# First pair's weight buffers refilled in halves, the last pair's up products ahead of the down products of the pair before, lambda and one GpSimd sum behind K's rotations

## The reference

```python
# first layer, differential attention
lam = exp(sum(lam_p[0] * lam_p[1])) - exp(sum(lam_p[2] * lam_p[3])) + lam_init
a = probs(q1, k1) - lam * probs(q2, k2)      # q and k normed and rotated (rope) before
# each layer's experts (expert e, its tokens)
xb  = x_pad[tok]
hid = silu(xb @ w1[e]) * (xb @ w3[e])        # w1, w3: 1024 x 512
y   = (hid @ w2[e]) * w                      # w2: 512 x 1024
```

## Time and profile before

| | |
|---|---|
| median of 3 runs | 2242.19 us (2239.77 to 2244.62) |
| the profiled execution | 2242.67 us, of which its span 2240.8 us |
| TensorE busy | 2118.8 us, 95% of the span |
| VectorE, ScalarE, GpSimd busy | 733.4, 387.8, 245.4 us |
| mean granted TensorE clock | 0.986 of full speed |
| DMA | 528.81 MB; mean 421 GB/s from 504 to 952 us and 426 GB/s from 1793 to 2185 us |
| chain that ended last | PE 79%, DMA 11%, DVE 5% |

### The profile page before, as it was taken

How to read it: one execution, slowest core, us unless ns; L and a number is a source line. 1 busy time by engine, 2 the same in 40 slices (tenths; PEclk the granted TensorE clock), 3 DMA queues, 4 the chain that set the end, 5 groups by cost and what they waited for, 6 DMA issues and landing times.

```text
span 2240.8 us, 27584 instructions
## 1 busy us (share of the span) xinstructions
PE 2118.8 (95%) x11803; PEld 1130.3 (50%) x11803; DVE 733.4 (33%) x1742; ACT 387.8 (17%) x742; POOL 245.4 (11%) x258
## 2 busy tenths in 40 slices
PE   9999899999998999989999999999999999998987
PEld 5454666654444433335556568764674533333332
DVE  3126675323001011041277864522232411111104
ACT  4001132121000100011133353210022100000001
POOL 6001211000000000000001142301110010000001
PEclk9999999999999999999998999999999999999999
DMA  8113104259999999995110021124352699999998
GB/s 300 50 38 113 50 26 169 83 208 389 424 422 428 427 421 427 428 391 179 29 30 2 3 77 39 64 87 150 113 225 94 237 421 427 428 428 427 427 425 334
DMA packets 96686, 528.81 MB, mean 236 GB/s; under 512 B 10286, under 2 KB 26339, under 8 KB 69162
## 3 DMA queue, kind: packets, MB, share of 16 engines
q1 hardware_dynamic: 82450, 492.11, 54.1%
q0 software_dynamic: 8160, 17.88, 2.2%
q10 hardware_dynamic: 5944, 16.94, 2.0%
HBM read 509.04 MB, written 30.41 MB: 241 GB/s over the span
## 4 chain that ended last, share of the span: by engine, by line
PE 79%; DMA 11%; DVE 5%; SPq 2%; ACT 1%; issue 1%; POOL 0%; DVEq 0%; POOLq 0%; ACTq 0%
PE ps L204 75%; DMA SC<-in_w_e_up 2%; DMA RING<-in_w_e_up 2%; DMA SC<-in_w_e_down 2%; SPq L1688 2%; DMA SC<-in_w 1%; DMA XT<-in_w 1%; DMA EX<-in_w_e_up 1%; DMA RING<-in_w 1%; PE ps L1774 1%; ACT SC L1931 1%; PE ps L1822 1%; PE ps L3349 0%; PE ps L2754 0%; DVE RING L3420 0%
## 5 line engine op out<-in xcount | busy, mean ns | idle before, releaser
L204 PE MATMUL ps<-SC 64*64 64x64 f32 (+5 forms) x5408 | 743.9, 348 | 46.7 <-ACT SC L1931 11.0
L204 PE MATMUL ps<-RING,SC 128*64 128x512 f32 (+2 forms) x1648 | 558.6, 587 | 22.7 <-ACT SC L1931 5.5
L204 PEld LDWEIGHTS ps<-SC 64*64 64x64 f32 (+2 forms) x5408 | 331.4, 146 | 343.9 <-issue 292.4
L204 PEld LDWEIGHTS ps<-RING,SC 128*64 128x64 f32 (+2 forms) x1648 | 192.6, 151 | 256.1 <-issue 245.5
L204 PE MATMUL ps<-XT,RING 128*128 128x256 f32 (+2 forms) x944 | 317.1, 489 | 3.0 <-DVE XT L200 1.6
L204 PEld LDWEIGHTS ps<-XT,RING 128*128 128x128 f32 (+1 forms) x944 | 176.2, 190 | 115.6 <-issue 100.4
L1999 DVE SCALAR_TENSOR_TENSOR SC<-ps,ST,SC 128x512 f32<-128x512 f32 x30 | 22.5, 751 | 643.2 <-PE ps L204 643.2
L204 PE MATMUL ps<-RING,XT 128*128 128x512 f32 (+1 forms) x384 | 147.8, 545 | 0.0
L204 PE MATMUL ps<-SC,RING 128*128 128x512 f32 (+2 forms) x504 | 134.6, 432 | 2.3 <-DVE SC L1270 0.8
L204 PE MATMUL ps<-XT,SC 128*64 128x512 f32 (+2 forms) x312 | 117.1, 528 | 2.0 <-DMA SC<-in_w_e_up 1.3
L204 PEld LDWEIGHTS ps<-RING,XT 128*128 128x128 f32 x384 | 69.5, 195 | 76.5 <-issue 75.8
(11 more groups left out here) (497 smaller groups left out, 1950.9 us busy)
## 6 DMA issues: line engine op xcount, KB each, us to landing
SC<-in_w SPq DMA_DIRECT2D x48, 2048.0 KB, 29.1
RING<-in_w SPq DMA_DIRECT2D x36, 2048.0 KB, 28.9
RING<-in_w_in SPq DMA_DIRECT2D x15, 2048.0 KB, 9.1
SC<-in_w_e_gate SPq DMA_DIRECT2D x14, 2048.0 KB, 40.9
SC<-in_w_e_up SPq DMA_DIRECT2D x13, 2048.0 KB, 41.7
SC<-in_w_e_down SPq DMA_DIRECT2D x13, 2048.0 KB, 37.5
RING<-in_w_e_gate SPq DMA_DIRECT2D x11, 2048.0 KB, 40.4
RING<-in_w_e_up SPq DMA_DIRECT2D x11, 2048.0 KB, 42.2
```

The costliest lines, as they stand in the source:

```text
L204: return e.matmul(out, l, r, start=st, stop=sp, skip_group_check=True)
```

## The change

Five edits.

1. `lam` moves on VectorE from ahead of K's rotations to behind them; its last two instructions (`lam_last`) and ScalarE's exponential go still further back, among the transposes of K.
2. In the string of mix1 one piece of G1 moves ahead of one of DF, and the first gate's sum S4 on GpSimd waits for M7, no longer for M6.
3. The refill of the first pair's slots: the loads `nfirst + 2` and `+ 3` are issued in halves, from the middle of the w3 products; `nfirst + 4` and `+ 5` in halves by columns, or by every second 512-column block, in pieces of 2 KB, from "down" 0 of the first pair.
4. The last pair's w1 and w3 are loaded ahead of pair 14's w2, and pair 14's w2 comes by columns, as the last pair's did and does. SyncE waits for the first halves of the last pair's w1 before it issues pair 14's w2 (both count on one semaphore).
5. TensorE does the last pair's `up_p` ahead of pair 14's "down"; the last pair's result goes to XG, since YS still holds pair 14's.

```diff
@@ -921,12 +921,12 @@
-            if tt == 3:
-                W.wait_ge(*c.on("l01"))
-                e.activation(df_l[:, 0:2], df_l[:, 0:2], AF.Exp).then_inc(*c.up("a", "el"))
             yield
         for src, dst, n in DFS:
             for h in range(4):
+                if n == "k" and h == 1:
+                    W.wait_ge(*c.on("l01"))
+                    e.activation(df_l[:, 0:2], df_l[:, 0:2], AF.Exp).then_inc(*c.up("a", "el"))
                 if h % 2 == 0:
...
@@ -941,6 +941,9 @@
+
+        def lam_last(e):
+            l = df_l
             W.wait_ge(*c.on("el"))
...
@@ -998,8 +1001,6 @@
             if tt == 2:
                 normed(e, df_k, "k")
-            if tt == 3:
-                lam(e)
...
@@ -1010,6 +1011,9 @@
                     rope(e, df_k, "k", h)
                     if h == 3:
                         c.also("v", "rope", "k")
+                        lam(e)
+                elif h == 2:
+                    lam_last(e)
...
@@ -1314,7 +1318,7 @@
         if first:
             first()
-        W.wait_ge(*c.on("M6", n))
+        W.wait_ge(*c.on("M7" if first else "M6", n))
         op(lambda p: m.S2[p], lambda p: w[:, 4:8, lo[p]], lambda p: m.S2[p], A.subtract, "S4", n)
 
...
@@ -1687,33 +1691,51 @@
-            put_n = 0
-            while put_n < 6 * NPAIR:
+            def columns():
+
+                loads = [put(n) for n in (put_n, put_n + 1)]
+                for hf in range(2):
+                    for label, free, dst, src in loads:
+                        for f in free if hf else [c.on("down", 0, 0)]:
+                            W.wait_ge(*f)
+                        part = (slice(None), slice(None), slice(512 * hf, 512 * hf + 512)) if label[2] == 2 else (slice(None), slice(hf, 8, 2))
+                        e.dma_start(dst[part], src[part]).then_inc(*slots.up(label))
+
+            turn = list(range(6 * LAST - 2)) + [6 * LAST + i for i in (0, 1, 2, 3, -2, -1, 4, 5)]
+            i_ = 0
+            while i_ < 6 * NPAIR:
+                put_n = turn[i_]
                 if put_n == 2 and bi == 0:
                     mk_s(e)
                 if bi == 0 and put_n in MV_LOADS:
                     mv_s(e, 1 - MV_LOADS.index(put_n))
-                if put_n == nfirst:
-                    halves(([c.on("half of w", 0, 0)], None), ([], None))
-                    put_n += 2
+                if put_n in (nfirst, nfirst + 2):
+                    halves(([c.on("half of w", 0, (put_n - nfirst) // 2)], None), ([], None))
+                    i_ += 2
+                elif put_n == nfirst + 4:
+                    columns()
+                    i_ += 2
                 elif put_n in (6 * LAST, 6 * LAST + 2):
                     j = put_n // 2 % 3
                     halves(([], lambda label: c.up(f"dh{j}", "half", LAST, j)), ([], None))
-                    put_n += 2
-                elif put_n == 6 * LAST + 4:
+                    i_ += 2
+                elif put_n in (6 * LAST - 2, 6 * LAST + 4):
+                    p_ = put_n // 6
                     loads = [put(n) for n in (put_n, put_n + 1)]
+                    if p_ < LAST:
+                        W.wait_ge(*c.on("half", LAST, 0))
                     for hf in range(2):
                         for label, free, dst, src in loads:
                             for f in () if hf else free:
                                 W.wait_ge(*f)
-                            e.dma_start(dst[:, :, 512 * hf:512 * hf + 512], src[:, :, 512 * hf:512 * hf + 512]).then_inc(*(slots.up(label) if hf else c.up("dh2", "half", LAST, 2)))
-                    put_n += 2
+                            e.dma_start(dst[:, :, 512 * hf:512 * hf + 512], src[:, :, 512 * hf:512 * hf + 512]).then_inc(*(slots.up(label) if hf else c.up("dh2" if p_ == LAST else "dh0", "half", p_, 2)))
+                    i_ += 2
                 else:
...
@@ -1793,8 +1815,9 @@
                 for k in range(8):
                     if k == 4:
+                        if picked:
+                            i.then_inc(*f.up("p", "half of w", q, j))
                         if picked and j == 0:
-                            i.then_inc(*f.up("p", "half of w", q, j))
...
@@ -1814,13 +1837,15 @@
-        def down_p(e, f, q, banks, w):
+        def ht_p(e, f, q, banks):
             b, free = banks("ht", q)
             W.wait_ge(*free)
             W.wait_ge(*f.on("hd", q))
             for j in range(4):
                 i = e.transpose(b[:, j * 128:(j + 1) * 128], HD.rearrange("p (c k) -> p k c", k=4)[:, j, :], ident[:, :])
             i.then_inc(*f.up("p", "ht", q))
+
+        def down_p(e, f, q, banks, w):
             W.wait_ge(*f.on("ev", "ht", q))
             for hf in range(2):
...
@@ -1841,7 +1866,7 @@
-                i = mm(e, b[:, :], hot2[:, tt * 128:(tt + 1) * 128], YS[:, hf * 512:(hf + 1) * 512], True, tt != 3)
+                i = mm(e, b[:, :], hot2[:, tt * 128:(tt + 1) * 128], XG[:, hf * 512:(hf + 1) * 512], True, tt != 3)
                 if tt < 3:
...
@@ -1866,7 +1891,7 @@
                 labels = [(f"m{bi}", q, j, x) for x in range(2)]
-                if q == LAST and not hf:
+                if not hf and (q == LAST or (q, j) == (LAST - 1, 2)):
                     W.wait_ge(*c.on("half", q, j))
...
@@ -1886,7 +1911,11 @@
-                down_p(e, c, q, c.take, w)
+                ht_p(e, c, q, c.take)
+                if q == LAST:
+                    down_p(e, c, LAST - 1, c.take, w)
+                if q != LAST - 1:
+                    down_p(e, c, q, c.take, w)
...
@@ -1924,16 +1954,22 @@
-        def down_a(e, f, q, at):
+        def ht_a(e, f, q, at):
             W.wait_ge(*f.on("ht", q))
             if f is c and q == 0:
                 W.wait_ge(*c.on("nov"))
+            if f is c and q == LAST:
+                W.wait_ge(*f.on("down", q - 1, 1))
             e.activation(HT, at("ht", q)[:, :], AF.Copy).then_inc(*f.up("a", "ev", "ht", q))
+
+        def down_a(e, f, q, at):
+            if f is c and q == LAST:
+                for hf in range(2):
+                    W.wait_ge(*f.on("down", q, hf))
+                    e.activation(XG[:, 512 * hf:512 * hf + 512], at("down", q, hf)[:, :], AF.Copy).then_inc(*f.up("a", "ev", "down", q, hf))
+                return
             if q >= 1 and f is c:
                 W.wait_ge(*f.on("y", q - 1))
-            if q == LAST and f is c:
-                W.wait_ge(*f.on("down", q, 0))
-                e.activation(YS[:, 0:512], at("down", q, 0)[:, :], AF.Copy).then_inc(*f.up("a", "ev", "down", q, 0))
             W.wait_ge(*f.on("down", q, 1))
...
@@ -1960,7 +1996,11 @@
-                down_a(e, c, q, c.at)
+                ht_a(e, c, q, c.at)
+                if q == LAST:
+                    down_a(e, c, LAST - 1, c.at)
+                if q != LAST - 1:
+                    down_a(e, c, q, c.at)
...
@@ -2308,9 +2349,11 @@
                     hotp_v(e, q + 2)
-                down_v(e, c, q, c.at)
+                if q < LAST - 1:
+                    down_v(e, c, q, c.at)
             hots_v(e)
             up_v(e, c, LAST, c.at)
+            down_v(e, c, LAST - 1, c.at)
             n_over = over(e)
...
@@ -2360,7 +2403,7 @@
 
-            W.wait_ge(*c.on("w", LAST - 1, 2))
+            W.wait_ge(*c.on("w", LAST, 0))
...
-            "hg*11 ho hg ho hg*3 df ho hg*6 df hg*3 df ho hg*3 df*3 hg ho hg df hg df*5 hg df hg*3 df g1 df*2 g1 df g1*3 df*3 dh "
+            "hg*11 ho hg ho hg*3 df ho hg*6 df hg*3 df ho hg*3 df*3 hg ho hg df hg df*5 hg df hg*3 df g1 df*2 g1*2 df g1*2 df*3 dh "
```

More of the change, by code:

```diff
@@ L1715, in s @@
                     e.dma_start(dst, src).then_inc(*slots.up(label))
-                    put_n += 1
+                    i_ += 1
             slots.put(hots_at, ("hot", bi), (c, ("add", NT - 1, 1)))
@@ L1910, in pair_p @@
                 up_p(e, o, q, banks, ow)
+                ht_p(e, o, q, banks)
                 down_p(e, o, q, banks, ow)
@@ L1972, in pair_a @@
                 up_a(e, o, q, fixed_at)
+                ht_a(e, o, q, fixed_at)
                 down_a(e, o, q, fixed_at)
```

## The result

The changed kernel took 2245.69 us in the median of 20 runs (2240.28 to 2250.68), against 2242.94 us of the kernel before in as many (2238.37 to 2245.87): ratio 1.0016, 95% interval 1.0008 to 1.0023, 3.6 us slower (1.8 to 5.2). The forecast was 1.0 us faster. The profiled execution took 2247.77 us, of which its span 2246.0; the span before was 2240.8. I cut both spans at places that both kernels have: the last 128x2048 product of K's norm on VectorE, the first product of dh, E (the landing of a stage's last weight), the last add of each stage, and the first gather of the second stage. The last two columns are differences after minus before.

What follows compares the result with a forecast made beforehand. Bounds: in mix1, TensorE waiting for VectorE's rotations of K; in the expert stages, DMA. Mix1 -5.7, stages +2.5 and +2.2 sum to -1.0 us: 2241.7, less 0.5 to the median, 2241.2 us; range 2235.5 to 2247.5.

Steps and rivals of the forecast that it cites:

- The tail: From E to the last add of each expert stage: E + 15.6 becomes E + 17.1, taken as +1.4 us a stage.
- the last table lands at E + 12.5 ... 3.6 and the last add 0.7 give E + 16.8: Stage end: after the late last table, TensorE's last eight products take 3.6 us and the last add 0.7.
- VectorE's E + 17.1: Stage end: VectorE can't start table 0 before E + 5.1, is then busy nearly throughout and ends at E + 17.1.
- Rival (b): Stage ends: SyncE's wait for pair 14's scatter delays all tables; 2249 us at 10.4 us, 2245 at 7.8; chance 0.15.
- my three signs of being wrong: Tables landing before TensorE asks for them, the scatter taking over 8 us, or S4 lying clear of the rotations.
- Mix1: Mix1, by moving lambda, M7 and S4: M5 at 252.6 instead of 259.01, gain 6.4 less 0.7 for the clock, -5.7 us.
- I cost its new place at nothing: Mix1: lambda behind K's rotations costs 0, being needed some 10 us later with only ScalarE's K copies queued behind its exponential.
- 3.5 of it is M7 that has gone into idle time, 1.7 is M7's slow clock: Mix1: the shares of the 6.4 us gain put down to M7 moving ahead of K's transposes.
- 1.3 us saved and 2 us of earlier products: Mix1: moving lambda saves 1.3 us on VectorE and brings TensorE's M1 and M6 about 2.1 us earlier.
- The refill and the load order: Expert stages: dips save 0.9 and 1.2 us, smaller pieces cost 2.0 a stage; E moves +1.1 and +0.8 us.
- its sum of 2.2 us less: Expert stages: with the skill page's 0.4 us instead of 0.95 for 4.19 MB in 2 KB pieces, total near 2239 us.

Runs made afterwards that it cites:

- late_tables: Kernel before, with SyncE issuing the four table loads only after the first half of the last pair's "down" products; ratio 1.0026.
- m7_only: Kernel before with only M7 moved ahead of K's transposes and S4 behind M7, lambda at its old place; mix1 30.9 us in one profile, ratio 0.9958 when timed.
- refill_only: Kernel before with only the new refill of the first pair's slots; ratio 0.9988.
- mix1_refill: Kernel before with both mix1 edits and the new refill of the first pair's slots, keeping the old tail; ratio 0.9965.

## Why the prediction was wrong

The forecast was -1.0 us, the measurement +3.6.

**The tail failed.** The step is "the last table lands at E + 12.5 ... 3.6 and the last add 0.7 give E + 16.8". Up to the scatter it was right: "down" 1 and both copies end where they should, the scatter starts at E - 5.0 and E - 4.5 (E - 4.9 was forecast) and lands in 5.4 and 5.1 us (5.9). From there two sizes are off. The last table lands at E + 13.6 and E + 14.5, 1.1 and 2.0 us late, and the last eight products take 5.4 us, not 3.6. That is 6.7 us in two stages against E + 16.8. The tails as forecast stood a little higher, on VectorE's E + 17.1, and were missed by 6.4. Rival (b) had the right mechanism, SyncE's wait for the scatter, and the wrong size: it took a slow scatter for the danger, and the scatter was quick. Its 2245 us, for a scatter of 7.8 us, is close to the measured 2245.69 by luck.

The tables' bytes moved as fast as forecast, except for the last of them. These are the packets from 2218.3 to 2229.5 us and from there to the landing:

```profile
DMA packets 546, 4.08 MB, mean 364 GB/s; under 512 B 48, under 2 KB 48, under 8 KB 48
DMA packets 171, 0.64 MB, mean 345 GB/s; under 512 B 31, under 2 KB 31, under 8 KB 155
```

By E + 11.7, 4.08 of the tables' 4.19 MB have moved. The last 0.1 MB takes 1.85 us more, while the DMA engines move 0.64 MB, mostly smaller pieces of the next load (the final norm's 0.5 MB, issued just behind the tables). In the first stage it is 4.04 MB by 997.6 and then 1.04 MB in 2.66 us, with w_ckv behind. What held back the last pieces of the tables no run separates.

The slow products come with that lateness. TensorE was ready for the table at E + 10.9, near the E + 10.8 that my terms give. A table at E + 12.5 would have left it idle for 1.7 us, and after 1.3 us late_tables had the full clock. At 2.78 and 3.48 us it had not. So the 3.6 us may have been right for my own landing time; I never asked what a later landing would do to the clock, though I had counted that price for mix1. VectorE, which I took for the last to finish, was done but for its last add at E + 17.1 in the second stage, and then waited 1.95 us for TensorE, whose path I had put 0.3 us below VectorE's. None of my three signs of being wrong came true, and the sum was wrong all the same: none of them asked for the time between the tables' issue and the last add.

Two slips in the sums change little: 17.1 less 15.6 is 1.5 and not 1.4, and (b) at 10.4 us is 2250 by its own terms and not 2249.

**Mix1: right place, wrong split.** M5 came at 252.8 for a forecast of 252.6. Lost there were 1.2 us of slow clock (0.7 was taken) and 0.8 us at dh, where "I cost its new place at nothing" failed: the work that is queued behind lambda's last two instructions is VectorE's copy for dh, and a GpSimd sum runs beside them. The Trainium skill (SBUF — State Buffer, "Who interferes with whom") says that a VectorE instruction with two inputs in SBUF and a GpSimd instruction that reads SBUF can't run together, and that the later one waits for the whole of the other instruction. The rows agree, 1.37 and 1.48 us instead of 0.41, and 0.92 for one element a partition. Larger is what I didn't ask: what M7's move would do without lambda's. "3.5 of it is M7 that has gone into idle time, 1.7 is M7's slow clock", 5.2 us, is most of the 6.6 of m7_only, and with M7 moved the lambda edit, which I counted as 1.3 us saved and 2 us of earlier products, took 2.3 to 3.1 away. Bringing the producer, TensorE's products ahead of S4, forward made the collision and the idle time.

**The refill and the load order.** The dips came back. In the second stage that gave 1.7 us to E (refill_only); the forecast had -1.2 and took about as much again for 2 KB pieces. In the first stage it gave nothing. The rate of 2 KB pieces is as in the earlier trace rows, 389 GB/s at 2209:2211, and the last pair's w2 takes 10.7 us, from 2207.04 to E, as forecast. Where the kernel without the columns was run beside one with them it was faster by 0.11% and 0.17%, 2.5 and 3.8 us where 1.9 were on record, but the intervals overlap widely and the distances to E differ by under 1 us in both directions. The smaller price of such pieces by the Trainium skill (DMA: Bandwidth & Descriptors, "Why small descriptors are slow") doesn't fit that rate: the rows have 8 to 9% where the estimate from the page was 4.7%. What the pieces cost the whole kernel, its sum of 2.2 us less or mine, these runs can't tell. Left open.

## What to carry to other kernels

A load that waits for the result of a step moves with that step: before reordering products, list what the DMA queue waits for behind them, and count from the wait to the last consumer, with the clock that TensorE has after the new idle time. Earlier work is not a gain when the engine it feeds is not late: with VectorE the last to finish in mix1, making TensorE earlier only brought GpSimd's sum onto the rotations. And test parts of a change alone and together; here the kernel with the lowest ratio leaves out edits 1, 4 and 5 and the columns of edit 3, and is 17 us faster than the whole by the ratios.

## What was not expected of the hardware

In mix2, which no edit touches, the stretch from the last add of the first stage to the second stage's gather took 770.6 us in one profiled execution and 782.3 in another. The granted clock makes most of the difference. First the kernel before, then refill_only, both from 1200 to 1240 us (columns as above):

```profile
1200.00:1220.00 20.00, 18.06 (x263) 11.62 (x261) 14.74 (x32) 7.14 (x12) 0.00 (x0) 0.82 0.01 2
1220.00:1240.00 20.00, 20.00 (x356) 14.20 (x357) 13.60 (x31) 5.80 (x13) 0.00 (x0) 0.75 0.01 2
```

```profile
1200.00:1220.00 20.00, 17.37 (x329) 11.38 (x328) 15.66 (x41) 8.72 (x17) 0.00 (x0) 1.00 0.01 2
1220.00:1240.00 20.00, 19.82 (x398) 11.84 (x398) 17.22 (x32) 6.04 (x11) 3.73 (x3) 1.00 0.01 2
```

TensorE's idle times ahead of it are alike, 0.35 and 0.78 us, before 1211.5 us in the one and before 1211 in the other. In the one the clock is at the lower level from about 1213 us on, for some 17 us (the rows miss 0.18 and 0.25 of 20 us, 8.6 us); in the other it stays. The two stretches differ by 8.0 us (778.6 and 770.6), more than most edits here, and the longest of all, 782.3 in mix1_refill, has a mean granted clock of 0.98 over it where refill_only has 1.00. So spans of single profiles must not be compared; stretches without mix2 can be, to about 1 us.
